# Attention's output projection as three rounded products, with its weights split ahead of it

## The chip, the cores and the metric

The kernel runs on one core of a Trainium2 chip. The metric is the time of one execution on the device in microseconds (us). Three runs of the kernel before took 1412.57, 1412.99 and 1413.47 us; their median is 1412.99 us.

## The reference, cut to what matters

A two-layer trunk over 256 tokens of width 1024: a gated DeltaNet with a dense SwiGLU, then sliding-window attention with a top-2-of-8 SwiGLU of experts. The change is in the second layer's attention, in the product with `w_o`:

```
q = (hn @ w_q) ...                                  # 16 heads of 64
s = q k_band + bias                                 # over a band of 192 keys
p = exp(s - m) / (sum(exp(s - m)) + exp(sink - m))
o = p v_band                                        # (256, 1024)
h = h + o @ w_o                                     # w_o: (1024, 1024)
hn = rms_norm(h, ffn_norm_w[1])                     # then router, top 2, experts
```

All inputs and the output are float32.

## The kernel before

The program is written by hand for each engine: `block.sync` (SyncE, which issues the large loads), `block.gpsimd`, `block.scalar`, `block.vector` and the tensor program. An engine works through its own list in order, and waits on semaphores for the others. No planner orders anything.

**Two ways of a float32 product.** Large products elsewhere (the q/k/v projection, the dense SwiGLU, the query projection) are done in three rounded products. An operand is split in two: ScalarE writes a rounded copy `hi` of type float32r, and VectorE or GpSimd writes `lo`, the operand less `hi`. The function `product` (lines 1640 to 1642) then issues three matmuls, hi by hi, hi by lo and lo by hi, into one accumulation. The attention's output projection, `merge` (line 2060), multiplies plain float32 instead; the trace shows two matmul records for each such call.

**The attention.** The 16 heads are taken in four groups of four (`g` 0 to 3). For each group:

- `scores(g)` on TensorE (line 2015) writes the scores into banks 0 to 2.
- `masked_scores(g)` on VectorE (line 1362) adds the bias and takes the maximum; lines 1368 and 1369 prepare the exponent's offset and release ScalarE.
- `exps(g)` on ScalarE (lines 909 and 911) takes 8 exponentials with their sums, and one for the sink.
- `weights(g)` on VectorE: lines 1375 and 1376 (denominator), then four multiplications of line 1380, one per chunk `n` of 64 queries.
- `values(g)` on TensorE: for each chunk `n` transposes (line 2029) into bank 6 or 7, which ScalarE copies out (lines 926 to 929, "the probability copies"), and one chunk behind them the products with the values (`heads`, line 2046) into bank 5.
- `heads_out(g)` on VectorE (line 1384) copies bank 5 into `oT`, the turned output. `values(g+1)` waits for it before it writes bank 5 again.

ScalarE's list is: `queries(0)`, `queries(1)`, `exps(0)`, `queries(2)`; then for each `g` the four chunks' probability copies, `exps(g+1)`, and for `g` 0 `queries(3)` (line 899, which scales the finished query projection out of its bank). VectorE's list is, for each `g`: `masked_scores(g)`, `heads_out(g-1)`, `weights(g)`; at the end `heads_out(3)`. TensorE's list is: `query(0)`, `query(1)`, `scores(0)`, `query(2)`, `scores(1)`, `values(0)`, `query(3)`, `scores(2)`, `values(1)`, `scores(3)`, `values(2)`, then the merges. `merge(t, kts, halves)` adds, for the 128 tokens of tile `t`, the blocks `kts` of the 1024 input channels into one or both 512-column halves of the output. Order: `merge(0, 0..5)`, `values(3)`, the rest of `merge(0)` and half 0 of `merge(1)`, transposes for the router, the first four blocks of `merge(1)` half 1, the router's product, the last four blocks, the transposes and the router for the second tile, and the expert selection (`top_two`, `first_gather`). In all 32 calls of 128x512. `s_aw` counts finished halves.

**The weights.** `w_o` is loaded as two halves of 2 MB into the slots 0 and 1 of `slot_space`, once the value projection has read slot 0 (semaphore `s_vmm2`) and two query groups slot 1 (`s_qmm` at 2). 

**The experts' ring.** Expert weights pass through eight ring slots of 1.75 MB, `ring0` to `ring7`, which lie over the slots and the workspace. The first eight loads (line 479) are for the first expert's gate and up rows, in pairs: pair `p` is read from rings `2p` and `2p+1`. In the kernel before, rings 0, 1 and 2 may be loaded once the query projection is done (`s_qmm` at 4), ring 3 at `s_aw` 3, and rings 4 to 7 at `s_aw` 4. After the first eight, each ring slot is loaded again as its last reader releases it. SyncE issues these loads in the order of its list.

Of the kernel before, what the change touches and what calls it, by code (L numbers as in the profile page):

```python
# [15 lines left out]
F32 = mybir.dt.float32  # L16
# [3 lines left out]
ALU = mybir.AluOpType  # L20
ACT = mybir.ActivationFunctionType
AX = mybir.AxisListType

P = 128
T, D = 256, 1024
NT, KT = T // P, D // P
# [106 lines left out]
def trunk(nc, ins, consts, cat, out):  # L133
    ctx = ExitStack()
    with ctx:
# [3 lines left out]
        def sem(name):  # L139
            return ctx.enter_context(nc.semaphore(name))  # L140


        slot0 = -(-nc.sbuf_base // 64) * 64
        slot_space = sb("slot_space", [P, 3 * KT * 512 + 16])
        slot = [nc.alloc_sbuf_tensor_at(f"weights{k}", [P, KT * 512], F32, offset=slot0 + 4 * k * KT * 512)
                for k in range(3)]
# [15 lines left out]
        ws0 = -(-nc.sbuf_base // 64) * 64  # L162
        ws = nc.alloc_sbuf_tensor_at("ws", [P, 28672], F32, offset=ws0)

        def rounded(name, words, at):
            return nc.alloc_sbuf_tensor_at(name, [P, words], F32R, offset=at)


        whi = [rounded(f"weights_hi{k}", 4096, ws0 + 4 * o_) for k, o_ in enumerate((20480, 16384, 8192))]
        wlo = [rounded(f"weights_lo{k}", 4096, ws0 + 4 * o_) for k, o_ in enumerate((24576, 12288, 4096))]  # L170

        ring = [nc.alloc_sbuf_tensor_at(f"ring{k}", [P, 2 * HALF], F32, offset=at)
                for k, at in enumerate((ws0 + 4 * 20480, ws0 + 4 * 24064, slot0 + 4 * 2 * KT * 512, slot0,
                                        slot0 + 4 * KT * 512, ws0 + 4 * 12288, ws0 + 4 * 15872, ws0 + 4 * 8704))]
        hT = [[nc.alloc_sbuf_tensor_at(f"hidden_turned{k}{b}", [P, HALF // 4], F32, offset=at) for b, at in enumerate(ats)]
              for k, ats in enumerate(([slot0 + 4 * (4096 * n + 3584) for n in range(3)],
                                       [ws0 + 4 * o_ for o_ in (19456, 19904, 27648)]))]
# [2 lines left out]
        qlo = [rounded(f"qkv_lo{k}", 4096, slot0 + 4 * k * KT * 512) for k in range(3)]  # L180
# [9 lines left out]
        xtl = rounded("x_lo", KT * T, ws0 + 4 * 2048)  # L190
        xqh = rounded("query_x_hi", KT * T, ws0 + 4 * 18432)
        xql = rounded("query_x_lo", KT * T, ws0)
        bank = [ctx.enter_context(nc.psum_tensor(f"bank{k}", [P, 512], F32)) for k in range(8)]
        xn_rows = nc.dram_tensor("xn_rows", (T + P, D), F32, kind="Internal").ap()
        h_rows = nc.dram_tensor("h_rows", (T + P, D), F32, kind="Internal").ap()
# [6 lines left out]
        def view(t, off, *dims):  # L202
            n = 1
            for d in dims:
                n *= d
            v = t[:, off:off + n]
            if len(dims) == 2:
                return v.rearrange("p (a b) -> p a b", b=dims[1])
            if len(dims) == 3:
                return v.rearrange("p (a b c) -> p a b c", b=dims[1], c=dims[2])  # L210
            return v
# [8 lines left out]
        def wide(ap, n):  # L220
            return ap.unsqueeze(2).to_broadcast([ap.shape[0], ap.shape[1], n])

        g8 = [view(s, 0, KT, 512) for s in slot]
# [40 lines left out]
        biasR = view(ws, 6144, PAIRS, BAND)  # L264
        bias = view(ws, 14848, PAIRS, BAND)
        sc = [view(ws, 9216 + 2048 * k, 2 * NC, T) for k in range(2)]
        oT = view(ws, 16384, KT, T)
        pT = [view(ws, 13312 + 512 * k, 4, P) for k in range(2)]

        e_act = view(ws, 0, 3, 2, 2 * PART)  # L270
# [101 lines left out]
        s_aw = sem("s_aw")  # L372
# [3 lines left out]
        s_rows, m_slot, m_next, m_now = (sem(n) for n in ("s_rows", "m_slot", "m_next", "m_now"))  # L376
        s_hback = sem("s_hback")
        m_rows, m_added, m_turn, m_free = (sem(n) for n in ("m_rows", "m_added", "m_turn", "m_free"))
        ring_in0, ring_in1, ring_in5, ring_in6, ring_in7 = (
            sem(n) for n in ("ring_in0", "ring_in1", "ring_in5", "ring_in6", "ring_in7"))  # L380
        ring_in = [ring_in0, ring_in1, loaded[2], loaded[0], loaded[1], ring_in5, ring_in6, ring_in7]
        m_gh, m_gu, m_d = (sem(n) for n in ("m_gh", "m_gu", "m_d"))
        m_act, m_hid, m_hT, m_y, m_sc, m_h = (sem(n) for n in ("m_act", "m_hid", "m_hT", "m_y", "m_sc", "m_h"))
        s_out = sem("s_out")
# [3 lines left out]
        PRE = [3, 3, 3]  # L388
        PRE_A = [n + NF for n in PRE]

        RING_PRE = [0, 0, PRE_A[2] + 1, PRE_A[0] + 2, PRE_A[1] + 2, 0, 0, 0]

        w_in, conv_w = ins["a_w_in"], ins["a_conv_w"]
        NATIVE = {0: 0, 2: 1, 4: 2}
# [33 lines left out]
        def _(sp):  # L428
# [46 lines left out]
            def e_load(k, dst, src, free, count):  # L475
                sp.wait_ge(free, count)
                if not isinstance(count, int):
                    sp.sem_inc(m_turn, 1)
                sp.dma_start(dst, src).then_inc(ring_in[k], 16)

            def e_in(w, x, hf, pair):
                return w[bass.ds(x, 1), pair * 256:pair * 256 + 256, hf * HALF:(hf + 1) * HALF].rearrange(
                    "e (k p) n -> p (e k) n", p=P)
# [6 lines left out]
            sp.sem_inc(m_d, 4)  # L490
            for pair in range(4):
                for w, k in ((mg, 2 * pair), (mu, 2 * pair + 1)):
                    e_load(k, r2[k], e_in(w, 0, 0, pair), *((s_qmm, 4) if k < 3 else (s_aw, 3) if k == 3 else (s_aw, 4)))
            for t in range(NT):
                sp.wait_ge(s_h, 8 + 2 * t + 2)
                sp.dma_start(h_rows[t * P:(t + 1) * P, :], h[:, t, :]).then_inc(s_rows, 16)
# [53 lines left out]
        def _(pool):  # L550
# [16 lines left out]
            def norm_rstd(k):  # L567
                r = rstd_of(k)
                for t in range(NT):
                    pool.wait_ge(s_ss, 4 * r + 2 * t + 2)  # L570
                    a = rs[:, r, t:t + 1]
                    link(pool.tensor_scalar(a, ss[:, r, t, 0:1], ss[:, r, t, 1:2], EPS, ALU.add, ALU.add))
                    pool.tensor_tensor(a, a, half2[:, 0:1], ALU.pow).then_inc(s_rstd, 1)
# [19 lines left out]
            for n in range(NC):  # L593
                pool.wait_ge(s_oss, n + 1)
                rstd(rso[:, n * JP:(n + 1) * JP], sso[:, n * JP:(n + 1) * JP],
                     half2[:, 0:JP], s_orstd, 1.0 / DH)
            for k in (1, 2, 4):
                norm_rstd(k)
                if k == 1:

                    pool.wait_ge(s_browc, 1)
                    pool.dma_start(bias_rows.ap(), view(ws, 18432, RELS + 1)[0:QH, :]).then_inc(s_bdram, 16)
                    pool.wait_ge(s_bdram, 16)
                    for hp in range(2):
                        pool.dma_start(biasR[hp * C:(hp + 1) * C, :, :],
                                       bass.AP(tensor=bias_rows, offset=hp * (RELS + 1),
                                               ap=[[1, C], [2 * (RELS + 1), PAIRS], [1, BAND]])).then_inc(s_bR, 16)
# [26 lines left out]
        def _(act):  # L634
# [262 lines left out]
            def queries(g):  # L897
                act.wait_ge(s_qmm, g + 1)
                act.activation(qT2[:, 2 * g:2 * g + 2, :], bank[3 + g % 2][:, :].rearrange("p (a b) -> p a b", b=T),
                               ACT.Copy, scale=HD ** -0.5).then_inc(s_qT, 1)  # L900

            def exps(g):
# [7 lines left out]
                                       accum_out=den[b][:, r:r + 1])  # L910
                act.activation(esk[b], esk[b], ACT.Exp).then_inc(s_exp, 1)

            queries(0)
            queries(1)
            exps(0)
            queries(2)
            for g in range(PAIRS // 2):
                for n in range(NC):
                    m = 4 * g + n
                    act.wait_ge(s_pt, m + 1)  # L920
                    nk = 1 if n < 2 else 2
                    w = C if n % 2 == 0 else P
                    src = bank[6 + m % 2][:, :].rearrange("p (a b) -> p a b", b=P)
                    dst = pT[m % 2]
                    if nk == 1 or w == P:
                        act.activation(dst[0:w, 0:2 * nk, :], src[0:w, 0:2 * nk, :], ACT.Copy).then_inc(s_pTc, 2)
                    else:
                        act.activation(dst[:, 0:2, :], src[:, 0:2, :], ACT.Copy).then_inc(s_pTc, 1)
                        act.activation(dst[0:w, 2:4, :], src[0:w, 2:4, :], ACT.Copy).then_inc(s_pTc, 1)
                if g < 3:  # L930
                    exps(g + 1)
                if g == 0:
                    queries(3)
            for t in range(NT):
                squares(4, s_h, 8, [t])
                turned(4, [2 * t])
# [59 lines left out]
        def _(dve):  # L996
# [383 lines left out]
                    dve.tensor_tensor(s_, s_, wide(rden[b][:, 2 * n:2 * n + 2], k1 - k0), ALU.mult).then_inc(s_p, 1)  # L1380

            def heads_out(g):
                dve.wait_ge(s_pv, g + 1)
                dve.tensor_copy(oT[:, 2 * g:2 * g + 2, :], view(bank[5], 0, 2, T)).then_inc(s_oT2, 1)

            for g in range(4):
                masked_scores(g)
# [202 lines left out]
        def _(pe):  # L1590
# [47 lines left out]
            def product(dst, ah, al, bh, bl, start, stop):  # L1638

                pe.matmul(dst, ah, bh, start=start, stop=False, skip_group_check=True)  # L1640
                pe.matmul(dst, ah, bl, start=False, stop=False, skip_group_check=True)  # L1641
                return pe.matmul(dst, al, bh, start=False, stop=stop, skip_group_check=True)  # L1642
# [410 lines left out]
            def merge(t, kts, halves=range(2)):  # L2053

                first, last = kts[0] == 0, kts[-1] == KT - 1
                for q in halves:
                    if first:
                        pe.wait_ge(loaded[q], 16 * (PRE_A[q] + 2))
                    for kt in kts:
                        m = pe.matmul(bank[2 * t + q][:, :], oT[:, kt, t * P:(t + 1) * P], g8[q][:, kt, :],  # L2060
                                      start=first and kt == kts[0], stop=last and kt == kts[-1],
                                      skip_group_check=True)
                    if last:
                        m.then_inc(s_aw, 1)

# [186 lines left out]
```

## Time and profile before

| | |
|---|---|
| median of three runs | 1412.99 us |
| the profiled execution | 1413.2 us |
| its span, first to last instruction | 1411.3 us |
| mean granted TensorE clock | 0.991 |
| TensorE matmul busy | 1377.0 us, 98% of the span |
| ScalarE, VectorE, GpSimd busy | 278.2, 500.8, 89.2 us |
| attention and routing, from the first query product to the first expert product | about 431.5 to 527.0 us |
| experts | from 527.0 us to about 1398 us |

Times in rows count from the start of the span. A matmul's record is longer than the distance to the next one, since matmuls are pipelined: the cost of a row of matmuls is read from their starts. ScalarE's and VectorE's records overlap a little in the same way.

### The profile page before, as it was taken

The page shows a single profiled execution, that of the slowest core. Times are in us where ns is not written, and L with a number is a line of the kernel's source. Part 1 is how long each engine was busy: PE and PEld are TensorE (multiplying, and loading weights), DVE is VectorE, ACT ScalarE, POOL GpSimd, SP SyncE. Part 2 cuts the span into 40 slices and gives each one's busy share as a digit, 9 for nine tenths or more (in the row PEclk, how much of TensorE's full clock was granted, in tenths as well). Part 3 has the DMA queues.
Part 4 walks back from the last instruction along what each step waited for, and adds up shares of the span by engine and source line. Part 5 has one row for each costly group of instructions (what it writes and reads, how often), then busy time and mean ns, then how long its engine had stood idle before and what let it go on. Part 6 is the DMA issues. An engine that isn't in the chain of part 4 may idle for free.

```text
span 1411.3 us, 31796 instructions
## 1 busy us (share of the span) xinstructions
PE 1377.0 (98%) x14487; PEld 759.1 (54%) x14487; DVE 500.8 (35%) x1030; ACT 278.2 (20%) x522; POOL 89.2 (6%) x75
## 2 busy tenths in 40 slices
PE   6999999999999989999999999999999999999997
PEld 6998967999989653333333333333333333333333
DVE  5767355555545346233042042042042141240222
ACT  5640134334455410000000000000000000000002
POOL 4340010000000000000100100100100100100000
PEclk8999999999999999999999999999999999999999
DMA  7542016555553359999999999999999999999991
GB/s 276 180 145 96 4 60 219 192 178 185 172 209 120 157 227 412 412 423 410 393 425 416 396 423 416 397 422 417 402 418 416 411 406 420 410 405 422 408 419 47
DMA packets 92987, 436.32 MB, mean 309 GB/s; under 512 B 5816, under 2 KB 29552, under 8 KB 84544
## 3 DMA queue, kind: packets, MB, share of 16 engines
q1 hardware_dynamic: 87232, 423.64, 75.2%
q0 software_dynamic: 3616, 7.42, 2.2%
q10 hardware_dynamic: 2016, 3.38, 0.7%
q8 instruction: 106, 1.74, 0.5%
q14 instruction: 17, 0.14, 0.0%
HBM read 427.46 MB, written 6.96 MB: 308 GB/s over the span
## 4 chain that ended last, share of the span: by engine, by line
PE 91%; DVE 4%; ACT 3%; DMA 1%; issue 1%; POOL 1%; POOLq 0%; DVEq 0%; ACTq 0%
PE bank L2168 41%; PE bank L2194 14%; PE bank L2197 7%; PE bank L1640 6%; PE bank L1641 6%; PE bank L1642 5%; PE bank L2060 2%; PE bank L1866 2%; PE bank L1676 1%; DVE ws L1053 1%; ACT qkv_hi L676 1%; PE bank L1781 1%; PE bank L1764 1%; PE bank L2046 1%; DMA weights<-in_a_w_in 1%
## 5 line engine op out<-in xcount | busy, mean ns | idle before, releaser
L2168 PE MATMUL bank<-ring,xt 128*32 128x448 f32 x6144 | 580.3, 539 | 0.4 <-DVE xt L1541 0.4
L2168 PEld LDWEIGHTS bank<-ring,xt 128*32 128x32 f32 x6144 | 199.5, 110 | 372.6 <-issue 369.7
L1492 DVE TENSOR_TENSOR ws<-ws,bank 64x448 f32<-64x448 f32 x96 | 82.3, 992 | 526.3 <-ACT ws L948 526.3
L2194 PE MATMUL bank<-ring,hidden_turned 128*32 128x512 f32 x1792 | 233.4, 592 | 0.0
L948 ACT ACTIVATE ws<-bank 64x448 f32<-64x448 f32 x96 | 51.9, 540 | 653.5 <-PE bank L2168 653.5
L2197 PE MATMUL bank<-ring,hidden_turned 128*32 128x256 f32 x1792 | 137.7, 379 | 0.0
L2197 PEld LDWEIGHTS bank<-ring,hidden_turned 128*32 128x32 f32 x1792 | 58.2, 110 | 134.0 <-issue 134.0
L1640 PE MATMUL bank<-x_hi,weights_hi 128*128 128x256 f32 x320 | 90.3, 282 | 1.3 <-issue 1.3
L1641 PE MATMUL bank<-x_lo,weights_hi 128*128 128x256 f32 x320 | 90.2, 282 | 0.0
L1642 PE MATMUL bank<-x_hi,weights_lo 128*128 128x256 f32 x320 | 89.4, 279 | 0.0
L1240 DVE TENSOR_TENSOR weights_lo<-weights,weights_hi 128x1024 fp32r<-128x1024 f32 x62 | 73.1, 1222 | 39.3 <-ACT weights_hi L797 39.3
L2194 PEld LDWEIGHTS bank<-ring,hidden_turned 128*32 128x32 f32 x1792 | 57.5, 110 | 42.3 <-issue 7.6
L797 ACT ACTIVATE weights_hi<-weights 128x1024 fp32r<-128x1024 f32 x62 | 62.1, 1051 | 56.2 <-PE bank L1642 56.2
L1499 DVE STREAM_TRANSPOSE hidden_turned<-ws 64x448 f32<-64x448 f32 x96 | 61.0, 636 | 2.7
L1640 PEld LDWEIGHTS bank<-x_hi,weights_hi 128*128 128x128 f32 x320 | 60.1, 188 | 1.9 <-issue 1.4
L1642 PEld LDWEIGHTS bank<-x_hi,weights_lo 128*128 128x128 f32 x320 | 60.8, 190 | 0.0
L1641 PEld LDWEIGHTS bank<-x_lo,weights_hi 128*128 128x128 f32 x320 | 60.3, 188 | 0.4
L1640 PE MATMUL bank<-qkv_x_hi,qkv_hi 128*128 128x256 f32 x192 | 56.7, 295 | 2.2 <-DVE qkv_x_lo L1035 2.2
L1641 PE MATMUL bank<-qkv_x_lo,qkv_hi 128*128 128x256 f32 x192 | 56.1, 292 | 0.0
L1642 PE MATMUL bank<-qkv_x_hi,qkv_lo 128*128 128x256 f32 x192 | 55.9, 291 | 0.0
L624 POOL DMA_INDIRECT h_rows<-ws,half_idx x7 | 11.0, 1568 | 650.2 <-ACT ws L969 560.7
L1053 DVE SCALAR_TENSOR_TENSOR ws<-bank,sm,ws 128x255 f32<-128x255 f32 (+2 forms) x72 | 34.7, 481 | 20.3 <-ACT ws L715 18.6
(338 smaller groups left out, 1373.2 us busy)
## 6 DMA issues: line engine op xcount, KB each, us to landing
ring<-in_moe_w_gate SPq DMA_DIRECT2D x64, 1792.0 KB, 13.6
ring<-in_moe_w_up SPq DMA_DIRECT2D x64, 1792.0 KB, 15.3
ring<-in_moe_w_down SPq DMA_DIRECT2D x64, 1792.0 KB, 14.6
weights<-in_a_w_in SPq DMA_DIRECT2D x7, 2048.0 KB, 9.0
weights<-in_ffn_w_up SPq DMA_DIRECT2D x11, 1024.0 KB, 5.4
weights<-in_ffn_w_gate SPq DMA_DIRECT2D x11, 1024.0 KB, 5.3
weights<-in_ffn_w_down SPq DMA_DIRECT2D x11, 1024.0 KB, 5.0
weights<-in_a_w_out SPq DMA_DIRECT2D x2, 2048.0 KB, 8.3
```

What stands on the lines that cost most here:

```text
L797: act.activation(hi[:, j * n:(j + 1) * n], slot[k][:, j * n:(j + 1) * n], ACT.Copy).then_inc(w_hi[k], 1)
L948: act.activation(e_act[0:C, b, c, :], bank[2 * b + c][C:P, 0:2 * PART], ACT.Silu).then_inc(m_act, 1)
L1053: i_ = dve.scalar_tensor_tensor(out=dst[:, sh:T], in0=src[:, 0:T - sh], scalar=cw[:, w:w + 1], in1=dst[:, sh:T], op0=ALU.mult, op1=ALU.add)
L1240: dve.tensor_tensor(to[:, c], slot[k][:, c], hi[:, c].bitcast(F32), ALU.subtract).then_inc(w_lo[k], 1)
L1492: dve.tensor_tensor(to, by_row[0], by_row[1], ALU.mult).then_inc(m_hid, 1)
L1499: dve.transpose(hT[k][b][C * u:C * u + C, :].rearrange("p (j l) -> p j l", l=LANE), blocks[:, u]).then_inc(m_hT, 1)
L1640: pe.matmul(dst, ah, bh, start=start, stop=False, skip_group_check=True)
L1641: pe.matmul(dst, ah, bl, start=False, stop=False, skip_group_check=True)
L1642: return pe.matmul(dst, al, bh, start=False, stop=stop, skip_group_check=True)
L2168: m = pe.matmul(by_run(bank[2 * b + c][LANE * g:LANE * g + LANE, 0:2 * PART]), xe[:, kt, LANE * b:LANE * b + LANE], w_[:, c, g % 2], start ...
L2194: pe.matmul(bank[6][LANE * g:LANE * g + LANE, :], hT[h][g // 2][:, r], moving(D * j + 512 * (g % 2), 512), start=begin, stop=end, skip_gro ...
L2197: m = pe.matmul(bank[7][LANE * q:LANE * q + LANE, 0:256], hT[h][2][:, r], moving(D * j + 256 * q, 256), start=begin, stop=end, skip_group_ ...
```

## The change

The projection goes through `product`. So `w_o` and the attention's output are each split:

- `out_weights(i, j)`: ScalarE rounds a quarter `j` of half `i` of `w_o` into `woh[i]`. The four quarters of half 0 stand one behind each of the four chunks' probability copies of `g` 0, those of half 1 likewise in `g` 1.
- GpSimd subtracts, in the same eight pieces, and writes the rest over the loaded weights in slot 0 and 1 (`wol`), ahead of its `norm_rstd(4)`.
- `heads_round(g)`: ScalarE writes the rounded copy of bank 5 (`oTh`), as the last thing of its turn `g`, behind `exps(g+1)` and, for `g` 0, behind `queries(3)`.
- `heads_out(g)`: VectorE waits for that copy instead of for TensorE, and writes bank 5 less `oTh` (`oTl`).
- `merge` waits for GpSimd's pieces and issues three matmuls for each of its 32 calls.
- The ring slots lie at other addresses, since `woh` and `wol` are in use longer: only ring 0 may be loaded at `s_qmm` 4, ring 1 at `s_pt` 16 (the last transposes of `values(3)`), rings 2 and 3 at `s_aw` 3, the others at `s_aw` 4 as before.

```diff
         ring = [nc.alloc_sbuf_tensor_at(f"ring{k}", [P, 2 * HALF], F32, offset=at)
-                for k, at in enumerate((ws0 + 4 * 20480, ws0 + 4 * 24064, slot0 + 4 * 2 * KT * 512, slot0,
-                                        slot0 + 4 * KT * 512, ws0 + 4 * 12288, ws0 + 4 * 15872, ws0 + 4 * 8704))]
+                for k, at in enumerate((slot0 + 4 * 2 * KT * 512, ws0 + 4 * 8704, slot0, ws0 + 4 * 20480,
+                                        slot0 + 4 * KT * 512, ws0 + 4 * 24064, ws0 + 4 * 12288, ws0 + 4 * 15872))]
...
+        oTh, oTl = rounded("attn_out_hi", KT * T, ws0 + 4 * 16384), rounded("attn_out_lo", KT * T, ws0 + 4 * 6144)
+        woh, wol = (whi[0], wlo[0]), (qlo[0], qlo[1])
...
-        RING_PRE = [0, 0, PRE_A[2] + 1, PRE_A[0] + 2, PRE_A[1] + 2, 0, 0, 0]
+        RING_PRE = [PRE_A[2] + 1, 0, PRE_A[0] + 2, 0, PRE_A[1] + 2, 0, 0, 0]
+        RING_FREE = ((s_qmm, 4), (s_pt, 16), (s_aw, 3), (s_aw, 3), (s_aw, 4), (s_aw, 4), (s_aw, 4), (s_aw, 4))
...
-                    e_load(k, r2[k], e_in(w, 0, 0, pair), *((s_qmm, 4) if k < 3 else (s_aw, 3) if k == 3 else (s_aw, 4)))
+                    e_load(k, r2[k], e_in(w, 0, 0, pair), *RING_FREE[k])
...
             for k in (1, 2, 4):
+                if k == 4:
+                    for piece in range(8):
+                        c = slice(1024 * (piece % 4), 1024 * (piece % 4) + 1024)
+                        pool.wait_ge(q_hi, 16 + piece + 1)
+                        pool.tensor_tensor(wol[piece // 4][:, c], slot[piece // 4][:, c], woh[piece // 4][:, c].bitcast(F32),
+                                           ALU.subtract).then_inc(q_lop, 1)
                 norm_rstd(k)
...
+            def out_weights(i, j):
+                c = slice(1024 * j, 1024 * j + 1024)
+                if j == 0:
+                    act.wait_ge(loaded[i], 16 * (PRE_A[i] + 2))
+                    act.wait_ge(s_qmm, 2 * i + 2)
+                act.activation(woh[i][:, c], slot[i][:, c], ACT.Copy).then_inc(q_hi, 1)
+
+            def heads_round(g):
+                act.wait_ge(s_pv, g + 1)
+                act.activation(view(oTh, 0, KT, T)[:, 2 * g:2 * g + 2, :], view(bank[5], 0, 2, T), ACT.Copy).then_inc(s_x0h, 1)
...
+                    if g < 2:
+                        out_weights(g, n)
                 if g < 3:
                     exps(g + 1)
                 if g == 0:
                     queries(3)
+                heads_round(g)
...
             def heads_out(g):
-                dve.wait_ge(s_pv, g + 1)
-                dve.tensor_copy(oT[:, 2 * g:2 * g + 2, :], view(bank[5], 0, 2, T)).then_inc(s_oT2, 1)
+                dve.wait_ge(s_x0h, 4 + g + 1)
+                v = lambda x: view(x, 0, KT, T)[:, 2 * g:2 * g + 2, :]
+                dve.tensor_tensor(v(oTl), view(bank[5], 0, 2, T), v(oTh).bitcast(F32), ALU.subtract).then_inc(s_oT2, 1)
...
                 for q in halves:
-                    if first:
-                        pe.wait_ge(loaded[q], 16 * (PRE_A[q] + 2))
+                    xh_, xl_ = (view(x, 0, KT, T)[:, :, t * P:(t + 1) * P] for x in (oTh, oTl))
+                    wh, wl = view(woh[q], 0, KT, 512), view(wol[q], 0, KT, 512)
                     for kt in kts:
-                        m = pe.matmul(bank[2 * t + q][:, :], oT[:, kt, t * P:(t + 1) * P], g8[q][:, kt, :],
-                                      start=first and kt == kts[0], stop=last and kt == kts[-1],
-                                      skip_group_check=True)
+                        if t == 0 and kt % 2 == 0:
+                            pe.wait_ge(q_lop, 6 + 4 * q + kt // 2 + 1)
+                        m = product(bank[2 * t + q][:, :], xh_[:, kt, :], xl_[:, kt, :], wh[:, kt, :], wl[:, kt, :],
+                                    first and kt == kts[0], last and kt == kts[-1])
```

## Rows read from the trace of the kernel before

**Rows 1.** The page's chain of work that ended last, by engine

```profile
PE 91%; DVE 4%; ACT 3%; DMA 1%; issue 1%; POOL 1%; POOLq 0%; DVEq 0%; ACTq 0%
```

**Rows 2.** The experts: page's group (busy, mean | idle), and SyncE's waits (us, times, longest)

```profile
L2168 PE MATMUL bank<-ring,xt 128*32 128x448 f32 x6144 | 580.3, 539 | 0.4 <-DVE xt L1541 0.4
...
SPq L479 <- PE bank L2168: 416.7, 50, 13.2
```

**Rows 3.** Timeline of TensorE over the attention: start, us, line, count [idle before]

```profile
453.56 0.62 PE L2029 MATMUL bank<-cst,ws 128*64 128x128 f32 x4
...
456.42 1.74 PE L2046 MATMUL bank<-ws 128*64 128x64 f32 x32
...
464.00 2.19 PE L2015 MATMUL bank<-ws 64*64 64x64 f32 x32
466.12 0.63 PE L2029 MATMUL bank<-cst,ws 128*64 128x128 f32 x4
...
470.66 2.19 PE L2015 MATMUL bank<-ws 64*64 64x64 f32 x32
473.85 0.77 PE L2029 MATMUL bank<-cst,ws 128*64 128x128 f32 x4 [1.00 <-DVE ws L1380]
...
478.38 10.57 PE L2060 MATMUL bank<-weights,ws 128*128 128x512 f32 x24
```

**Rows 4.** Timeline of TensorE, first and last of 48 rounded 512-column matmuls

```profile
401.54 0.39 PE L1640 MATMUL bank<-weights_hi,hidden_hi 128*128 128x512 f32 x1
...
412.19 0.39 PE L1642 MATMUL bank<-last_down_hi,last_hidden_lo 128*128 128x512 f32 x1
```

**Rows 5.** Groups by shape: the projection's matmuls (425 to 530 us), the page's weight rounding

```profile
L2060 PE MATMUL bank<-weights,ws 128*128 128x512 f32 x64 | 28.4, 597 | 0.0
...
L797 ACT ACTIVATE weights_hi<-weights 128x1024 fp32r<-128x1024 f32 x62 | 62.1, 1051 | 56.2 <-PE bank L1642 56.2
```

**Rows 6.** Timeline of ScalarE over the attention

```profile
454.06 0.65 ACT L926 ACTIVATE ws<-bank 64x256 f32<-64x256 f32 x2 [1.92 <-PE bank L2029]
...
457.08 0.34 ACT L909 ACTIVATE ws<-ws,sm 128x64 f32<-128x64 f32 x1
...
460.27 0.20 ACT L911 ACTIVATE sm<-sm 128x8 f32<-128x8 f32 x1
...
469.16 0.60 ACT L926 ACTIVATE ws<-bank 128x512 f32<-128x512 f32 x1 [0.38 <-PE bank L2029]
```

**Rows 7.** Timeline of VectorE over the attention

```profile
473.06 0.17 DVE L1375 TENSOR_TENSOR sm<-sm 128x8 f32<-128x8 f32 x1 [1.60 <-ACT sm L911]
...
473.50 1.57 DVE L1380 TENSOR_TENSOR ws<-ws,sm 128x128 f32<-128x128 f32 x4
...
478.50 0.69 DVE L1384 COPY ws<-bank 128x512 f32<-128x512 f32 x1 [0.72 <-PE bank L2046]
```

**Rows 8.** GpSimd's split of weights (by shape), and GpSimd beside VectorE (timelines)

```profile
L580 POOL TENSOR_TENSOR qkv_lo<-weights,qkv_hi 128x2048 fp32r<-128x2048 f32 x6 | 27.9, 4656 | 47.7 <-ACT qkv_hi L676 44.6 <-ACT qkv_hi L689 3.1
...
97.03 1.91 POOL L588 TENSOR_TENSOR ws<-cst,sm 128x1024 f32<-128x1024 f32 x1 [0.29 <-DVE sm L1094]
...
97.19 1.77 DVE L1097 TENSOR_TENSOR sm<-sm 128x16 f32<-128x16 f32 x1
```

**Rows 9.** Stretches: us, busy (count) of PE, PEld, DVE, ACT, POOL; PEclk, DMA, GB/s

```profile
84.00:87.00 3.00, 3.00 (x110) 3.00 (x108) 1.45 (x3) 1.42 (x5) 2.60 (x1) 1.00 0.69 197
88.00:91.00 3.00, 3.00 (x18) 3.00 (x17) 2.05 (x6) 0.78 (x2) 0.00 (x0) 0.55 0.95 361
...
519.00:525.00 6.00, 4.95 (x24) 4.85 (x24) 2.21 (x14) 1.25 (x3) 0.00 (x0) 0.50 1.02 430
...
470.00:476.00 6.00, 4.83 (x76) 3.54 (x72) 3.56 (x16) 3.92 (x19) 0.00 (x0) 1.00 1.02 424
```

**Rows 10.** Timelines of SyncE's issues and of TensorE, at the first expert

```profile
503.90 0.37 SPq L479 DMA_DIRECT2D ring<-in_moe_w_up  x1
...
527.02 18.25 PE L2168 MATMUL bank<-ring,xt 128*32 128x448 f32 x192 [0.39 <-DVE xt L1541]
```

More of the change, by code:

```diff
@@ L266, in trunk @@
         sc = [view(ws, 9216 + 2048 * k, 2 * NC, T) for k in range(2)]
-        oT = view(ws, 16384, KT, T)
         pT = [view(ws, 13312 + 512 * k, 4, P) for k in range(2)]
@@ L378, in trunk @@
         m_rows, m_added, m_turn, m_free = (sem(n) for n in ("m_rows", "m_added", "m_turn", "m_free"))
-        ring_in0, ring_in1, ring_in5, ring_in6, ring_in7 = (
-            sem(n) for n in ("ring_in0", "ring_in1", "ring_in5", "ring_in6", "ring_in7"))
-        ring_in = [ring_in0, ring_in1, loaded[2], loaded[0], loaded[1], ring_in5, ring_in6, ring_in7]
+        ring_in1, ring_in3, ring_in5, ring_in6, ring_in7 = (
+            sem(n) for n in ("ring_in1", "ring_in3", "ring_in5", "ring_in6", "ring_in7"))
+        ring_in = [loaded[2], ring_in1, loaded[0], ring_in3, loaded[1], ring_in5, ring_in6, ring_in7]
         m_gh, m_gu, m_d = (sem(n) for n in ("m_gh", "m_gu", "m_d"))
```

## The prediction

> **What bounds the kernel now.** I read the chain of waits first: TensorE holds 91% of it [rows 1]. The experts take two thirds of the time, and there TensorE waited 0.4 us in 6144 records, while SyncE's loads waited 416.7 us for TensorE [rows 2]. So the experts are bound by TensorE and not by the transfers; they keep their length, and what counts is when they begin. I then read the attention engine by engine. TensorE is fed almost without a pause: of the four softmax groups only `values(2)` was waited for, 1.00 us for VectorE's line 1380, at 473.85 [rows 3]. That pause is the thing to hold on to: the chain probability copies, `exps(2)`, `weights(2)`, `values(2)` is already the late one. Whatever the change puts on ScalarE or VectorE there is paid in full.
>
> **The gain.** The 32 calls of `merge` are 64 records [rows 5]. 24 of them take 10.57 us, less the last one's own 0.60, over 23 distances: 0.43 us each, 0.86 per call [rows 3]. A rounded matmul of the same shape, with its weight load, comes every (412.19 - 401.54) / 47 = 0.227 us [rows 4], so 0.68 for three. Gain: 32 x 0.18 = 5.8 us. I take it whole: the shape, the operand types and the order of the three products are those of rows 4. Bounds: 0.24 us for a distance would leave 4.5 us; the plain record's 0.43 halved, 0.215, would give 6.9.
>
> The Trainium skill (FP8 and Floating Point Precision, TensorE Precision Notes) says that true FP32 takes four passes through the array. By that a call would be 4 x 0.227 = 0.91 us and the gain 7.2. The trace has two records of 0.43 in place of four passes of 0.227; I keep the rows' 5.8.
>
> **What it costs, group by group.** A rounding of 128x1024 on ScalarE is a record of 1.05 us [rows 5]; consecutive records overlap by about 0.1 (two copies in 0.65 us, [rows 6]), so 0.95 in a row. A probability copy of a chunk is 0.28 (256 columns) or 0.5 to 0.56.
>
> `g` 0. The first copy begins 0.5 us after `values(0)` (454.06 against 453.56, [rows 3, 6]). Three roundings now stand ahead of the last copy. Before, ScalarE paused between copies for TensorE, and those pauses hide part: the last copy begins at 454.06 + 0.28 + 0.28 + 0.56 + 3 x 0.95 = 458.0, where it would have begun 0.5 ahead of 457.08. So `values(0)` ends 1.4 us later, and `exps(1)` begins at 458.0 + 0.5 + 0.95 = 459.5 and ends 3.4 later (457.08 to 460.47, [rows 6]), 462.9. That is not what ends last. `scores(2)` began at 464.00 [rows 3], so `query(3)` now ends at 465.4. Behind it, on ScalarE, stand `queries(3)` and then `heads_round(0)`, each a bank of 512 columns like the 0.60 us copy [rows 6]: done at 466.5. VectorE waits there, with `weights(1)` queued behind: 0.69 for the subtraction (as the copy it replaces, [rows 7]), then 0.79 from line 1375 to TensorE's start (473.06 to 473.85, [rows 3, 7]). `values(1)` begins at about 468.1, not 466.12: **+2.0**.
>
> `g` 1. `exps(2)` began 3.5 us after `values(1)` (469.16 + 0.5 against 466.12, [rows 3, 6]). With four roundings the last copy begins at +0.5 + 1.12 + 2.85 and `exps(2)` 1.45 later, at +5.9: 2.4 more, all on the late chain. **+2.4**. After `exps(2)`, at 477.4, come `heads_round(1)` (0.5) and the subtraction (0.7) before `weights(2)`: where `heads_out(1)` once lay beside the exponentials it now lies behind them. **+1.2**.
>
> GpSimd. Its 128x2048 subtraction is 4.66 us [rows 8], so a piece is 2.3. Four pieces run from 455.4 to 464.7, beside VectorE work that is done. The other four run from about 470 to 479, and there VectorE prepares `exps(2)` and starts `weights(2)`. The trace shows what that does: a VectorE subtraction of 16 columns, some 0.17 us alone, took 1.77 us and ended as GpSimd's 1.91 us operation did [rows 8]. A VectorE operation with both inputs in SBUF that meets a piece waits for its end. Line 1369 at about 472 or line 1375 at 478.6 meets one; from the slack at either I take **+0.6**. Bounds: 0, and two whole pieces, 4.6. The Trainium skill (SBUF — State Buffer, Who interferes with whom) says the same: a VectorE instruction with two SBUF inputs contends with a GpSimd instruction that reads SBUF. By that the copies from PSUM and line 1362 go free, and the sum is the same +0.6.
>
> `values(2)` thus begins near 480.0 instead of 473.85: **+6.2**. `values(1)` ends 5.9 us after its start of 468.1 (last copy begun at +4.5, 0.6 long, then its products), `scores(3)` takes 2.19 [rows 3]: TensorE is done at about 476.2 and then stands idle 3.8 us.
>
> `g` 2 and 3. No roundings. `heads_round(2)` and the subtraction are done some 8.6 us after `values(2)` begins, while `merge(0, 0..3)` runs until +10; `weights(3)` is done at +10.6, ahead of `values(3)` at +12.7. `heads_out(3)` becomes 1.4 us of two engines, covered by the two calls of `merge(1)` in front (1.36): 0. TensorE's waits on `q_lop` cost nothing: the last piece is done near 479.5, the merge begins near 484.6; were GpSimd 5 us later, the merge, with `values(3)` behind it, would wait. `norm_rstd(4)`, queued behind the pieces, is due near 500.
>
> **The clock.** It fell to half after TensorE did only tiny matmuls (110 records in 3 us, 84 to 87), and stayed low for about 3 us; and it was at half through 519 to 525, with TensorE partly idle; it stayed at full with the pause of 1.00 us inside 470 to 476 [rows 9]. The new idle of 3.8 us is longer than that. If it falls, some 3 us run at 1.2 GHz; dense work would lose 1.5, the short matmuls of `values(2)` less. I take **+0.8**. Bounds: 0 and 3.0 (half of six us, as at 519 to 525).
>
> **The ring.** Rings 2 and 3 are now issued at `s_aw` 3, as ring 3 was at 503.90 [rows 10]; the page's time to landing is 13.6 to 15.3 us, so 519. Pair 0 is read from 527.02, and 192 records in 18.25 us are two pairs, so pair 1 is due at 536 [rows 10]. Cover 17 us. Rings 0 and 1 land earlier still; the last four are issued as before. SyncE's new wait on `s_pt` holds up only loads that wait longer anyway. 0 us. Without that cover each late load would be paid as it is.
>
> **Sum.** 6.2 - 5.8 + 0.8 = +1.2 on the profiled 1413.2 (span 1411.3 plus 1.9 around it): 1414.4. The profiled run stands 0.2 above the median, so **1414.2 us**: no change that can be told. What a measurement of this kernel can tell is about 0.2%, 2.8 us.
>
> **The rivals.**
> - *The half clock reaches the merges (slower).* The idle ahead of `values(2)` takes the clock down, and its short matmuls do not bring it back before the merges. For: in 519 to 525 it stayed low twice as long [rows 9]. Against: 470 to 476, with as thin work, stayed at full. It decides once the idle passes the pauses seen here. 1413.0 + 6.2 - 5.8 + 3.0 = 1416.4. Chance 0.14.
> - *GpSimd holds VectorE twice (slower).* Lines 1368, 1369 and 1375 each wait a whole piece: 4.6 in place of the 0.6, and 0.8 of clock: 1413.0 + 5.6 + 4.6 - 5.8 + 0.8 = 1418.2. For: rows 8. Against: `exps(2)` waits for ScalarE's roundings at that time anyway. 0.08.
> - *The stalls are absorbed (faster).* If the roundings fall into ScalarE's pauses and only +2.5 of the late chain remains: 1413.0 + 2.5 - 5.8 = 1409.7. For: ScalarE's and VectorE's low busy share. Against: the late chain has no pause but TensorE's 1.00 us. 0.08.
> - *Three products are no faster than the plain one here.* 1413.0 + 6.2 + 0.8 = 1420.0. Against: rows 4. 0.03.
>
> **Range and chances.** The forecast, within 0.2%, has 0.64. The unknown costs reach from 1410.5 (full gain of 6.9, no contention, no clock) to 1418.0 (the first two rivals, in part), which leaves out fewer than 2 in 10. The forecast's own range is 1411.5 to 1416. Faster by over 0.2%: 0.09 (the third rival and a little). Same: 0.66. Slower: 0.25.
>
> **What would show it.** `values(1)` starting near 468, `values(2)` near 480 with an idle of 3 to 4 us ahead, released by VectorE; 96 records of lines 1640 to 1642 about 0.227 us apart in the merges; the first expert product at 527 to 530; the experts' length the same to 0.5 us; no wait for a ring. I am wrong if `values(2)` starts before 477 (the late chain was misread), if merges stand at `q_lop`, or if the experts' length changes.

## The result, and the profile after

The kernel after took **1417.65 us** (median of 7 runs, 1417.16 to 1418.12) against 1413.24 us for the kernel before (7 runs, 1411.87 to 1414.06): a ratio of 1.0031, 95% interval [1.0021, 1.0041]. That is 4.4 us slower where 1.2 was forecast. The time lies 0.35 us inside the widest bounds given (1410.5 to 1418.0) and outside the forecast's own range (1411.5 to 1416), and it is not "no change": it is the side that had a chance of 0.25.

The profiled execution took 1418.12 us, span 1416.2 us, mean granted clock 0.989. I read it in the order of the prediction. First the experts, in the page's costliest groups of after:

```profile
L2192 PE MATMUL bank<-ring,xt 128*32 128x448 f32 x6144 | 580.3, 539 | 0.4 <-DVE xt L1564 0.4
```

Its busy time, count and idle time are those of [rows 2]: the experts kept their length, and no expert product waited for a ring. So the loss lies ahead of them. Then the timeline of TensorE after (start, us, engine, line, and in brackets the idle time before and its releaser), which answers to [rows 3]:

```profile
467.26 0.77 PE L2052 MATMUL bank<-cst,ws 128*64 128x128 f32 x4 [0.42 <-DVE ws L1402]
...
470.89 1.12 PE L2069 MATMUL bank<-ws 128*64 128x64 f32 x16 [0.45 <-ACT ws L948]
472.32 0.98 PE L2069 MATMUL bank<-ws 128*64 128x64 f32 x16 [0.30 <-ACT ws L945]
473.23 3.48 PE L2038 MATMUL bank<-ws 64*64 64x64 f32 x32
479.20 1.03 PE L2052 MATMUL bank<-cst,ws 128*64 128x128 f32 x4 [2.49 <-DVE ws L1402]
...
486.29 0.80 PE L1663 MATMUL bank<-weights_hi,attn_out_hi 128*128 128x512 f32 x1
486.88 0.63 PE L1664 MATMUL bank<-qkv_lo,attn_out_hi 128*128 128x512 f32 x1
487.31 0.63 PE L1665 MATMUL bank<-weights_hi,attn_out_lo 128*128 128x512 f32 x1
...
489.44 0.46 PE L1664 MATMUL bank<-qkv_lo,attn_out_hi 128*128 128x512 f32 x1
489.74 0.39 PE L1665 MATMUL bank<-weights_hi,attn_out_lo 128*128 128x512 f32 x1
...
531.87 1.33 PE L2192 MATMUL bank<-ring,xt 128*32 128x448 f32 x12 [0.39 <-DVE xt L1564]
```

`values(2)` starts 5.35 us later than before, after a pause of 2.49 us. It then takes 7.09 us (479.20 to 486.29) where it took 4.53 (473.85 to 478.38, [rows 3]). The first merges stand 0.43 us apart, nearly twice the distance of [rows 4]; from 489.74 on they stand 0.233 apart. The stretches of after name the reason (us; then busy time and count of PE, PEld, DVE, ACT, POOL; the granted clock; DMA share; GB/s):

```profile
470.00:472.00 2.00, 1.55 (x20) 0.99 (x18) 1.93 (x8) 2.00 (x5) 2.00 (x2) 1.00 0.48 201
472.00:474.00 2.00, 1.70 (x30) 1.57 (x30) 1.88 (x1) 1.30 (x3) 2.00 (x2) 0.63 0.03 8
474.00:476.00 2.00, 2.00 (x18) 1.66 (x16) 0.00 (x0) 2.00 (x11) 2.00 (x1) 0.52 0.00 0
476.00:478.00 2.00, 0.71 (x10) 0.31 (x6) 0.18 (x1) 1.78 (x8) 2.00 (x2) 1.00 0.00 0
478.00:480.00 2.00, 0.80 (x4) 0.43 (x4) 1.93 (x7) 0.17 (x1) 0.46 (x1) 0.84 0.00 0
480.00:482.00 2.00, 1.97 (x16) 1.21 (x16) 2.00 (x14) 0.59 (x2) 0.00 (x0) 0.50 0.00 0
...
486.00:488.00 2.00, 2.00 (x12) 1.60 (x9) 0.00 (x0) 2.00 (x10) 0.00 (x0) 0.50 0.00 0
488.00:490.00 2.00, 2.00 (x7) 1.54 (x7) 1.78 (x6) 0.11 (x1) 0.00 (x0) 0.60 0.00 0
```

A clock of 0.50 is the lower of the two levels, 1.2 GHz in place of 2.4. It was granted twice: once during the short matmuls of `scores(3)` (3.48 us long in place of 2.19, but TensorE would have waited anyway: without it the pause ahead of `values(2)` would have been 3.78 us, the idle of 3.8 that was forecast), and again from about 479.3 to 489.4, some 10 us. No pause over 0.45 us stands ahead of the first fall. The kernel before stayed at 1.00 through all of this.

The ledger of the two profiled executions, up to the first expert product (531.87 against 527.02, +4.85). Its last line is the remainder and not a measurement of its own:

| | us |
|---|---|
| `values(2)` starts later (479.20 against 473.85) | +5.35 |
| `values(2)` itself at the low clock (7.09 against 4.53) | +2.56 |
| first merges at the low clock: 8 distances in 3.45 us, 1.96 at the full clock (e3 below) | +1.49 |
| routing, last merge to experts (14.89 against 14.34); the clock was low there for 10 us, 7 before | +0.55 |
| what is left for the merges' gain | -5.10 |

### The profile page after: what moved, and what is told of

It reads as the page before. It is cut to its first block, busy times and chain, and to the rows that moved or that the text cites. A ratio compares the mean times of both kernels' runs of the same rounds, so it can differ in the third digit from the quotient of the medians.

```text
span 1416.2 us, 31886 instructions
## 1 busy us (share of the span) xinstructions
PE 1381.3 (98%) x14519; PEld 772.0 (55%) x14519; DVE 503.0 (36%) x1030; ACT 287.6 (20%) x534; POOL 108.0 (8%) x83
## 4 chain that ended last, share of the span: by engine, by line
PE 90%; DVE 4%; ACT 3%; issue 1%; POOL 1%; DMA 0%; POOLq 0%; DVEq 0%; ACTq 0%
PE bank L2192 41%; PE bank L2218 14%; PE bank L2221 7%; PE bank L1663 6%; PE bank L1664 6%; PE bank L1665 6%; PE bank L1889 2%; PE bank L1699 1%; DVE ws L1075 1%; ACT qkv_hi L684 1%; PE bank L1804 1%; PE bank L1787 1%; PE bank L1803 1%; PE bank L1997 1%; PE bank L2069 1%
```

## The experiments

**e1: the ring alone.** The kernel before, with the new slots' addresses, semaphores and release points.

```
-  ... *((s_qmm, 4) if k < 3 else (s_aw, 3) if k == 3 else (s_aw, 4)))
+  RING_FREE = ((s_qmm, 4), (s_pt, 16), (s_aw, 3), (s_aw, 3), (s_aw, 4), ...)
+  ... *RING_FREE[k])
```

> The kernel before with only the ring slots' new addresses and their new conditions; the projection stays plain. Theory (the stall of the softmax chain and the half clock after it make the whole +4.4 us): no change, 1413.2 within 0.5 us, values(2) at about 473.8, the experts 873.3 us long. Rival (the ring costs: later first loads, or addresses that PE reads more slowly): part of the +4.4 is here, 1414.5 or more, with a longer experts' stage or a wait for the first ring slots.

Measured: 1412.38 us, ratio 0.9995 [0.9986, 1.0003]. The ring costs nothing that these runs can tell. The profiled execution was the slowest of the 11, 1415.0, and it taught something. Its timeline of TensorE:

```profile
473.08 0.77 PE L2030 MATMUL bank<-cst,ws 128*64 128x128 f32 x4 [1.00 <-DVE ws L1381]
...
475.36 1.11 PE L2030 MATMUL bank<-cst,ws 128*128 128x128 f32 x4
```

The pause is the old 1.00 us, yet the third set of transposes takes 1.11 us in place of 0.66: the clock fell in the middle of `values(2)` (0.61 on average through 474 to 480). `values(2)` took 6.02 us (473.08 to 479.10) for 4.53, and the first 24 records of the merges 12.09 for 10.57: 3.0 us, about what this run lies above the median. So with this pause the fall is possible; the other ten runs are at least 1.4 us faster than this one.

**e2: no split of the weights.** After, without `out_weights` on ScalarE and without GpSimd's pieces. No split of `w_o` exists then: both parts of the weights are read from the tiles `whi[0]` and `wlo[0]`, which hold other weights, so the projection's values are left out of the computation and only its time is kept.

```
-                    if g < 2:
-                        out_weights(g, n)
-        woh, wol = (whi[0], wlo[0]), (qlo[0], qlo[1])
+        woh, wol = (whi[0], wlo[0]), (whi[0], wlo[0])
```

> The changed kernel without the weights' split: ScalarE's eight roundings and GpSimd's eight subtractions are left out, and the three products read the rounded query weights in their place (so the output projection's values are not the reference's). The attention's output is still split. Theory: values(1) begins 0.5 us later than in the kernel before, values(2) 1.6 later (the rounding and subtraction behind exps(2)), the clock stays at 2.4 GHz, the merges gain 5.5: 1413.2 + 1.6 - 5.5 = 1409.4, within 1 us. Rival (the split of the attention's output, not that of the weights, is what costs): 1414 or more.

Measured: 1413.87 us, 12 runs from 1409.91 to 1416.45, ratio 1.0002 [0.9992, 1.0012]. Two runs (1409.91 and 1409.95) meet the expected 1409.4; ten lie 2.9 to 6.5 us above them. That the two kept the clock is not shown: their mean granted clock over the whole execution is 0.990, as in three of the ten. One of the ten was profiled (1413.93); its TensorE timeline and its stretches:

```profile
475.05 0.89 PE L2044 MATMUL bank<-cst,ws 128*64 128x128 f32 x4 [2.52 <-DVE ws L1394]
...
482.02 0.80 PE L1655 MATMUL bank<-weights_hi,attn_out_hi 128*128 128x512 f32 x1
```

```profile
474.00:480.00 6.00, 4.90 (x36) 3.25 (x36) 4.84 (x25) 1.91 (x6) 0.00 (x0) 0.63 0.00 0
480.00:486.00 6.00, 6.00 (x38) 4.72 (x37) 2.05 (x7) 3.85 (x19) 0.00 (x0) 0.52 0.00 0
```

What the pause of 2.52 us has over the old 1.00 now comes from the heads' split alone, and `values(2)` takes 6.97 us. Taking the weights' work away bought its own time and left the clock's price.

**e3: the pause filled.** After, with 10 rounded matmuls of 512 columns in TensorE's pause, into a bank that holds nothing that is still needed.

```
+            def filler(n):
+                for k in range(n):
+                    pe.matmul(bank[3][:, :], view(oTh, 0, KT, T)[:, k % 2, 0:P], view(woh[0], 0, KT, 512)[:, k % 8, :], ...)
...
             scores(3)
+            pe.wait_ge(s_qT, 4)
+            pe.wait_ge(s_oT2, 1)
+            filler(10)
             values(2)
```

> The changed kernel with ten idle rounded 128x512 matmuls into a bank not in use, between scores(3) and values(2), in TensorE's pause; about 2.3 us at 2.4 GHz, so they end about as values(2) may begin. Theory: the half clock from 479 to 489 costs 4.1 us (values(2) 7.1 us for 4.5, fourteen matmuls 0.43 apart for 0.23) and comes from TensorE's pause; with the pause filled it does not come: 1417.7 - 4.1 = 1413.6, within 1 us, values(2) to the first merge in 4.5 us. Rival (the clock is set by the thin work of values(1) before it, or the price is not the clock's): 1417.5 to 1419.

Measured: 1416.26 us, ratio 1.0017 [1.0009, 1.0026], in two groups: five runs at 1413.98 to 1414.42 and six at 1416.26 to 1418.53. The profiled one (1414.42) is of the first group. TensorE's timeline, then a stretch:

```profile
474.85 2.56 PE L2092 MATMUL bank<-weights_hi,attn_out_hi 128*128 128x512 f32 x10
479.00 0.78 PE L2052 MATMUL bank<-cst,ws 128*64 128x128 f32 x4 [1.59 <-DVE ws L1402]
...
483.53 0.50 PE L1663 MATMUL bank<-weights_hi,attn_out_hi 128*128 128x512 f32 x1
```

```profile
480.00:486.00 6.00, 6.00 (x67) 4.73 (x68) 2.85 (x19) 4.54 (x19) 0.00 (x0) 1.00 0.00 0
```

`values(2)` starts within 0.2 us of after's, and takes 4.53 us again, as before. More work on TensorE, and the kernel is 3.5 us faster in that group (its median of 1414.14 against 1417.65), as expected; over all eleven runs it is 1.4. The other group was not profiled. Its mean granted clock over the whole execution is 0.987 in three runs and 0.991 to 0.992 in three, against 0.992 to 0.994 in the first group: in part of it the clock was low for longer, but where is not shown.

**e4: VectorE does the heads' rounding too**, in place of ScalarE, so that the rounding does not stand behind the exponentials.

```
-                act.activation(view(oTh, 0, KT, T)[:, 2 * g:2 * g + 2, :], view(bank[5], 0, 2, T), ACT.Copy).then_inc(s_x0h, 1)
...
+                dve.wait_ge(s_pv, g + 1)
                 v = lambda x: view(x, 0, KT, T)[:, 2 * g:2 * g + 2, :]
+                dve.tensor_copy(v(oTh), view(bank[5], 0, 2, T)).then_inc(s_x0h, 1)
```

> The changed kernel with the attention's output rounded by VectorE, just before its subtraction, and no longer by ScalarE behind the exponentials. So heads_out lies beside exps again. Theory: values(1) begins as scores(2) ends (0.45 us earlier), values(2) 1.65 us earlier than in the changed kernel: 1417.7 - 1.65 = 1416.0 if the clock still falls, 1412 if the shorter pause keeps it up. Rival (VectorE's extra 0.69 us per group costs as much as it frees): 1417.7.

Measured: 1417.49 us (7 runs, 1417.03 to 1420.69), ratio 1.0028 [1.0017, 1.0039]. Next to nothing. The profiled execution is the slowest of them (1420.69). Its timeline of VectorE, then of GpSimd:

```profile
473.07 0.69 DVE L1405 CAST attn_out_hi<-bank 128x512 fp32r<-128x512 f32 x1 [1.50 <-PE bank L2069]
473.80 0.69 DVE L1407 TENSOR_TENSOR attn_out_lo<-bank,attn_out_hi 128x512 fp32r<-128x512 f32 x1
476.55 1.96 DVE L1395 TENSOR_TENSOR sm<-sm 128x8 f32<-128x8 f32 x1 [2.06 <-ACT sm L919]
```

```profile
469.18 9.30 POOL L604 TENSOR_TENSOR qkv_lo<-weights,weights_lo 128x1024 fp32r<-128x1024 f32 x4 [4.27 <-ACT weights_lo L926]
```

The heads are done early, at 474.5, as meant. But `weights(2)` now comes at 476.55, still beside GpSimd's last piece, and its first instruction ends with that piece (478.5) after 1.96 us in place of 0.17. What the edit gave, GpSimd took; `values(2)` started at 479.12 after a pause of 3.98 us, and the clock fell.

**e5: the roundings in ScalarE's pauses.** Those of the first half of the columns go around `exps(0)`, `queries(2)` and behind `exps(1)`, those of the second half behind `exps(3)`, and the merges are ordered anew, first half first.

```
             queries(1)
+            out_weights(0, 0)
             exps(0)
             queries(2)
+            out_weights(0, 1)
...
-                    if g < 2:
-                        out_weights(g, n)
                 if g < 3:
                     exps(g + 1)
                 if g == 0:
+                    out_weights(0, 2)
+                    out_weights(0, 3)
                     queries(3)
+                if g == 2:
+                    for n in range(4):
+                        out_weights(1, n)
```

> The changed kernel with the weights' roundings moved into ScalarE's pauses: one piece of half 0 before exps(0), one after queries(2), two after exps(1), all four of half 1 after exps(3); and the merges reordered so that the twelve calls before values(3) all use half 0. Theory: values(1) begins 0.6 us later than in the kernel before, values(2) 1.75 later, no GpSimd piece meets VectorE's preparation of exps(2), the clock stays up: 1413.2 + 1.75 - 5.5 = 1409.5, within 1 us. Rival (GpSimd's pieces beside weights(0), weights(1) and weights(3) hold VectorE as they held it before exps(2), and the merges wait at q_lop): 1412 to 1415.

Measured: 1417.76 us (9 runs, 1414.59 to 1418.69), ratio 1.0027 [1.0017, 1.0037]. My expectation failed. `values(2)` did start early, at 476.08, but behind a pause of 2.53 us, and the clock fell at about 478.4, in the middle of it. Then, in its timelines of TensorE and VectorE:

```profile
476.08 0.77 PE L2057 MATMUL bank<-cst,ws 128*64 128x128 f32 x4 [2.53 <-DVE ws L1407]
...
494.27 0.44 PE L2057 MATMUL bank<-cst,ws 128*128 128x128 f32 x2 [1.94 <-DVE ws L1407]
...
497.34 2.76 PE L2074 MATMUL bank<-ws 128*64 128x64 f32 x32
```

```profile
487.73 0.69 DVE L1412 TENSOR_TENSOR attn_out_lo<-bank,attn_out_hi 128x512 fp32r<-128x512 f32 x1 [7.73 <-ACT attn_out_hi L930]
...
489.51 5.64 DVE L1407 TENSOR_TENSOR ws<-ws,sm 128x128 f32<-128x128 f32 x4
```

The second half's roundings kept `heads_round(2)` waiting on ScalarE, and GpSimd's four pieces made `weights(3)` 5.64 us long, 1.57 alone. So `values(3)` had a pause of its own, 1.94 us, and the clock fell a second time: the last row's 32 matmuls take 2.76 us in place of 1.74.

**e6: e4 and e5 together.**

> The pauses' kernel (roundings of weights in ScalarE's pauses, merges reordered) and VectorE rounding the attention's output. Theory: nothing is left on the late chain: values(2) within 0.3 us of the kernel before, merges 5.5 us shorter: 1413.2 - 5.5 + 0.3 = 1408.0, within 0.7 us, faster than both kernels. Rival (a pause or a low clock appears elsewhere, as after the routing's thin work): 1410 or more.

Measured: **1408.57 us** (6 runs, 1407.44 to 1410.32), ratio 0.9966 [0.9954, 0.9978]: faster than both kernels, by 4.6 and 9.1 us. Its timeline of TensorE and one stretch:

```profile
474.30 0.78 PE L2057 MATMUL bank<-cst,ws 128*64 128x128 f32 x4 [1.00 <-DVE ws L1405]
...
478.83 0.50 PE L1668 MATMUL bank<-weights_hi,attn_out_hi 128*128 128x512 f32 x1
...
487.34 0.60 PE L2057 MATMUL bank<-cst,ws 128*64 128x128 f32 x4
...
522.98 11.48 PE L2200 MATMUL bank<-ring,xt 128*32 128x448 f32 x120 [0.39 <-DVE xt L1569]
```

```profile
480.00:486.00 6.00, 6.00 (x28) 4.82 (x27) 4.53 (x7) 5.45 (x13) 3.32 (x2) 1.00 0.01 3
```

The pause is back at 1.00 us, `values(3)` has none, and the clock is 1.00 throughout 462 to 498. The two edits alone gave -0.2 and +0.1 us; together -9.1. Each alone left one pause of 2.5 us or more.

**e7: the pause alone, in the kernel before.** VectorE repeats one small reciprocal of `weights(2)`.

```
+                if g == 2:
+                    for _ in range(12):
+                        link(dve.reciprocal(rden[b], den[b]))
```

> The kernel before, with nothing of the change: VectorE repeats the reciprocal of weights(2) 12 times (the same values are written again), at 0.20 to 0.24 us each, so values(2) begins some 2.6 us later and TensorE's pause ahead of it grows from 1.00 to some 3.6 us. If the pause alone takes the granted clock down: 2.6 + 3 to 4 for the short matmuls and the first merges at 1.2 GHz = 1419 to 1420, with the clock at 0.50 in some 10 us from about 476. If the pause costs only its own length (the clock falls for another reason that belongs to the change): 1415.8, clock 1.00 throughout 462 to 498.

Measured: 1419.69 us (5 runs, 1418.57 to 1420.85), ratio 1.0043 [1.003, 1.0057]: 6.2 us (the kernel before took 1413.49 beside it) for 2.81 us of repeats. Timelines of VectorE and TensorE, and a stretch:

```profile
473.19 2.81 DVE L1379 RECIPROCAL sm<-sm 128x8 f32<-128x8 f32 x12
```

```profile
476.38 1.06 PE L2032 MATMUL bank<-cst,ws 128*64 128x128 f32 x4 [3.85 <-DVE ws L1383]
...
480.89 2.76 PE L2049 MATMUL bank<-ws 128*64 128x64 f32 x32
```

```profile
480.00:486.00 6.00, 6.00 (x39) 3.84 (x40) 1.94 (x8) 3.87 (x18) 0.00 (x0) 0.50 0.00 1
```

Nothing of the change is in this kernel. The pause costs its own length and 3.4 us more, as `values(2)` (7.20 us, 476.38 to 483.58) and the first merges run at 1.2 GHz.

**e8: e2 with e3's filler.**

```
             scores(3)
+            filler(10)
             values(2)
```

> The kernel of e2 (the weights' split left out, second product on unsplit weights; heads split and three products kept) with the 10 filler matmuls of e3 ahead of values(2); they write a bank that is not read. If the clock is what ate the gain: all runs near the two fastest of e2, 1409.9, ratio 0.9977, clock 1.00 in 462 to 498, no two clusters. If the gain of the three products is smaller than worked out: 1413.9 as in e2 (the filler lies in the pause and costs nothing).

Measured: 1409.35 us, ratio 0.9972 [0.9961, 0.9983]; seven runs lie between 1408.77 and 1410.32, in one group. Its profiled execution took 2895.14 us, about twice that, for a cause that is open, so no trace shows the clock of this stretch. The mean granted clock over the whole of each of the seven is 0.994 in five, 0.991 and 0.990 in two, against 0.985 to 0.990 in e2. Ten matmuls whose result nobody uses make e2 4.5 us faster, and what is left is 4.1 us under the kernel before (1413.49 beside it): the gain of the three products less what the heads' split costs.

**e9: only half of GpSimd's pieces.** After, without the four for columns 512 to 1023 (the second product of that half reads another tile in their place).

```
-                    for piece in range(8):
+                    for piece in range(4):
```

> After, without GpSimd's four subtractions for output columns 512 to 1023 (the second product of that half reads another tile in their place: that part of the computation is left out). ScalarE's roundings stay. If GpSimd's contention is the small cost read from the trace (ScalarE waited 0.70 us for VectorE's line 1391): 0.7 us less, 1417.0, values(2) still after a pause of 1.8 us; if such a pause keeps the clock, some 4 us less in part of the runs, down to 1413. If GpSimd costs two pieces (4.6 us): 1413.0 with values(2) at 474.6.

Measured: 1416.97 us (10 runs), ratio 1.0024 [1.0015, 1.0034], against 1417.65 for after. The 0.7 us are as the small reading had it, but the two ratios' intervals overlap, so the times alone only exclude the two whole pieces. The trace says more: from the start of `scores(2)` to that of `values(2)` it is 13.74 us (464.80 to 478.54) where after has 14.55 (464.65 to 479.20), still with 3.27 us of idle at its end (here `scores(3)` had run at the full clock), and the clock was 0.50 through 480 to 486.

Side by side (pause ahead of `values(2)` and granted clock of 480 to 486, profiled execution; time, median):

| kernel | pause, us | clock | time, us |
|---|---|---|---|
| before | 1.00 | 1.00 | 1413.24 |
| e6 | 1.00 | 1.00 | 1408.57 |
| e1, profiled execution alone | 1.00 | 0.82 | 1415.0 |
| e3, filled | 1.59 | 1.00 | 1414.14 (5 of 11 runs; all: 1416.26) |
| after | 2.49, low clock in `scores(3)` | 0.50 | 1417.65 |
| e2 | 2.52 | 0.52 | 1413.87 |
| e5 | 2.53 | 0.56 | 1417.76 |
| e9 | 3.27 | 0.50 | 1416.97 |
| e7 | 3.85 | 0.50 | 1419.69 |
| e4 | 3.98 | 0.50 | 1417.49 |

The stretch is a fixed one. The clock was low for about 10 us in after and e2, some 7 in e1, e5 and e9, and over 13 in e4 and e7.

## Why the prediction was right or wrong

**The gain of the merges, -5.8: right in kind, a little less.** 0.231 to 0.233 us from product to product, not 0.227 (in e3, 29 distances in 6.70 us). 32 x (0.867 - 0.696) = 5.5; the ledger leaves 5.1. e6 gives the same without a remainder: its first twelve calls take 8.51 us (478.83 to 487.34), where they took 10.41 before (478.38 to 488.79), so 0.158 a call and 5.1 for 32, since the first product of a row comes later than the others.

**`values(1)` at 468.1, +2.0: near.** 467.26. The profiled execution of after ran 0.5 us ahead of before's from `scores(1)` on, so the delay was 1.6.

**`values(2)` at 480.0, +6.2: near.** 479.20, and with the same 0.5 the delay was 5.85. The idle ahead of it was 2.49 us and not 3.8, because `scores(3)` itself ran at the low clock and ended later. Roundings, heads behind the exponentials and the order of the engines came as worked out.

**GpSimd, +0.6: right, by a narrow margin.** Timeline of VectorE after, then of ScalarE:

```profile
470.81 0.74 DVE L1390 TENSOR_SCALAR sm<-sm 128x8 f32<-128x8 f32 x1
471.59 2.28 DVE L1391 TENSOR_TENSOR sm<-sm 128x8 f32<-128x8 f32 x1
```

```profile
473.91 0.35 ACT L917 ACTIVATE ws<-ws,sm 128x64 f32<-128x64 f32 x1 [0.70 <-DVE sm L1391]
```

The rival was half there: both instructions ended with a piece of GpSimd's, after 0.74 and 2.28 us in place of 0.17 each (0.17 each again in e9, without those pieces). ScalarE's roundings hid all but 0.70, and in e9's trace 0.8 came back. The Trainium skill (SBUF — State Buffer, Who interferes with whom) calls the ports that VectorE shares with GpSimd an exclusive lock, and says that the order of issue decides who blocks. The trace agrees: in e4 a VectorE instruction of 8 columns that began during GpSimd's last piece ended with it, at 478.5, after 1.96 us.

**The ring, 0, and `heads_out(3)`, `q_lop`, `norm_rstd`, 0: right.** e1, and no such wait in after.

**The lower bound.** The prediction puts 1410.5 beside "full gain of 6.9, no contention, no clock"; its own terms give 1413.0 + 5.6 - 6.9 = 1411.7. Nothing measured hangs on it.

**The clock, +0.8: this is the step that failed.** The prediction said that "if it falls, some 3 us run at 1.2 GHz; dense work would lose 1.5, the short matmuls of `values(2)` less". It fell, but for some 10 us: `values(2)` lost 2.56 and the first merges 1.49, 4.05 together. The short matmuls lost more than half of their own time again, and they did not bring the clock back; it came back only some 3 us into the merges. In addition the routing stage lost 0.55, which no term had. With 4.05 in place of 0.8, 5.85 for 6.2, 5.1 for 5.8 and the 0.55, the sum is +5.35; less the 0.5 of the head start that is +4.85, the ledger's figure. The first rival named just this mechanism, and gave it 0.14 and 3.0 us. Both were too small; its own sum, 1416.4, is 1.2 short. So the time stayed within the widest bounds because their upper end was drawn from the rivals, and not because the forecast's terms held. I had taken the length from [rows 9], where a fall lasted some 3 us with dense 512-column work behind it. The other stretch of [rows 9], 519 to 525, with thin work, was the nearer one, and I held it for the exception.

That the pause is the cause, and no property of the three products or of the ring, is shown by three runs: e7 makes the same fall in the kernel before with nothing but a longer pause; e3, in the profiled execution, keeps the clock with the pause filled; e6 keeps it with the pause at its old length. e8 agrees by its times. A long pause is not the only way to a fall, though: after's own first one, in `scores(3)`, had only pauses up to 0.45 us ahead of it, and e3, e4 and e9 went through the same stretch at 1.00; e1 fell behind the old 1.00 us. The pause makes likely what now and then comes without it.

The Trainium skill (TensorE: Matmul & The Clock Gate, What's actually happening) says that the gate follows how busy the array has been recently, and that the hardware's look at it runs free of the kernel's start. The groups of run times in e2 and e3, and the fall in e1 with the old pause, are what such chance would give; which of its matmuls a run caught it on, no run here shows.

**What stays open.** Why e3's second group is 2 to 4 us slower, and what set apart the two shortest runs of e2. Between which pauses the fall becomes the rule: 1.00 us mostly kept the clock, e3's 1.59 behind the filler kept it, and e5's 1.94 ahead of `values(3)` was followed by a fall. And whether e4's price of 4 us of pause shows the whole of GpSimd's hold: its profiled execution was 3 us above its median.

## What to carry to other kernels

When a change makes TensorE wait longer between short matmuls, price the pause by its length and then by what follows it. Here pauses of 2.5 us and more in place of 1.0 cost 3.4 to 4.5 us beyond their length (e7, and e2 against e8), because thin work after it ran at 1.2 GHz until dense work had run for a while. Where such a pause can't be avoided, filling it with idle matmuls may be worth more than the edit that caused it; where two engines share its cause, undo both, since one alone may buy nothing.

## What the runs showed of the hardware

- Useless matmuls made two kernels faster: 4.5 us in e8 against e2, 3.5 us in the better group of e3.
- A pause of 1.00 us mostly kept the clock (before, e6), but not always (e1's profiled execution, 2.6 us above its median). After's clock first fell, from about 472.5 to 475.9, with no pause over 0.45 us ahead of it.
- At the low clock the rounded 512-column matmuls stood 0.43 us apart, at the full clock 0.233; four small transposes took 1.11 us against 0.66.
- GpSimd's pieces of 2.33 us stretched VectorE's four multiplications of 1.57 us to 5.64 (e5) and its 8-column instructions of 0.17 us to 1.96 (e4) and 2.28 (after).
